# A diffusion-block kernel's head: x on the weights' queue, silu(c) and the norm factor in PSUM, fewer modulation tiles ahead of the first normed tile

## The chip, the cores and the metric

One core of one Trainium2 chip (trn2) runs the program. The metric is device microseconds of one execution, the median of several. Engines are called by their names or by the profile's short ones: TensorE (PE), VectorE (DVE), ScalarE (ACT), GpSimd (POOL), SyncE (SP, here only a DMA queue).

## What is computed

Two transformer blocks, one behind the other, on 512 tokens of width 1024, with a context of 256 tokens in the second. The head of the first block is what matters here:

```python
c_act = jax.nn.silu(c)
mod = c_act @ w_ada[l] + b_ada[l]
sh1, sc1, gt1, sh2, sc2, gt2 = [m[:, None, :] for m in jnp.split(mod, 6, axis=-1)]
h = rms_norm(x, g_norm1[l]) * (1.0 + sc1) + sh1
proj = h @ w_in[l]
qa, ka, va, qb, kb, vb, gates = jnp.split(proj, split_at, axis=-1)
```

`rms_norm` divides by the root of the mean square over the 1024 channels. Behind it come two attentions, gates, an output projection and a feed-forward part, then two further layers with their own modulation (`layer` 1 and 2 of the code).

## The kernel before

`build_program` writes a list of steps, `plan`, in one order. Each engine walks the whole list and issues its own part of each step, so an engine's order is the plan's order; waits on semaphores are placed from tokens that each step carries. x lies transposed in SBUF, channels on partitions: `XL` is 8 tiles of 128 channels x 512 tokens.

Products are made in three terms. Each weight unit of 128x1024 fp32 is loaded into one of three `RAW` buffers, ScalarE writes its rounded high part `SHI` (L2072), POOL the low part `SLO` (L2242), and TensorE issues high x high, high x low, low x high (L2505 to L2507). `with_splits` puts a unit's split into the plan: for the first three units at the places `first_splits`, which the head notes behind squares 1, 3 and 5, for later units where the buffer's former unit is released. `load_order` sorts what SyncE's queue issues: modulation tiles and weight units by a number `at`, plan positions for other transfers of that queue. At the start x, c and CONST (which holds the matrix of ones) go over ScalarE's queue, and tiles and units over SyncE's.

A **modulation tile** is 128 of the 6144 outputs of `c_act @ w_ada`. Its 128x1024 weights are loaded into `ADA` or `early` buffers, and one VectorE operation (L2321) multiplies them by the broadcast silu(c) and sums along the row, with a small read of the accumulator behind it. A pair of tiles, shift k and scale k, is wanted for channel tile k.

The head runs as follows. ScalarE makes silu(c) (L2067), then squares the eight x tiles (L2076), with the first three unit splits between them. TensorE sums all squares with a matrix of ones (L2497). ScalarE makes the factor r in two steps (L2080, L2082). `started` issues modulation pairs and then, for each k: `Coef` (L2326), `f = x * coef * r` (L2306, VectorE), `HLh` (L2086, ScalarE), and one step later `HLl` (L2311, VectorE). Then `v_tiles` multiplies: for each k, 4 token blocks x 3 terms, 96 instructions in all, two k to a weight unit. Its four banks are copied into `vb` (`VCopy`), two by ScalarE (L2091) and two by VectorE (L2332), and the query and key projections follow.

Pairs 0 to 4 are issued ahead of k = 0, and pair k + 5 ahead of `Coef` k for k = 0, 1, 2. Two pools of PSUM banks exist: 4 to 7 are handed out by `take`, 0 to 3 belong to the attention scores and are unused in the head.

## Time and profile before

| | us |
|---|---|
| median of 3 runs | 2798.8 (2796.88 to 2801.44) |
| profiled execution, its own time | 2794.1 |
| profiled execution, span | 2791.8 |
| TensorE busy | 2618.6 |
| VectorE, ScalarE, GpSimd busy | 1558.8, 1102.8, 983.8 |
| first instruction of the value projection | 39.75 |
| last instruction of it, start | 62.80 |

The profiled execution's own time contains 2.3 us outside its span. All times of day below are microseconds from the span's start. Busy time of a waiting engine's neighbours tells little: an engine's idle time matters only if TensorE, which is busy most of the span, waits for it.

### The profile page before, as it was taken

Reading aid. Unit: us, or ns where it says so; the run is one execution under the profiler, and the core shown is the slowest. Engines: PE = TensorE matmul, PEld = TensorE weight load, DVE = VectorE, ACT = ScalarE, POOL = GpSimd, SP = SyncE. Lnnn points to the kernel's source line nnn. Section 1 sums busy time; section 2 is a strip of 40 time slices with the busy share of each in tenths; the row PEclk is TensorE's granted clock in tenths of the full one; section 3 lists DMA queues with packets and bytes.
Section 4 is the critical chain, followed back from the end, with each engine's and each line's share of the span. In section 5 each row is a group of like instructions: output and inputs, shape, how many; then the busy total and the mean of one; then the engine's idle time right before and its main releaser. Section 6 shows DMA issues by size and latency. Waiting matters only on the chain. (4 is left out here: it accounts for less than half of the span.)

```text
span 2791.8 us, 39434 instructions
## 1 busy us (share of the span) xinstructions
PE 2618.6 (94%) x15254; PEld 2191.6 (78%) x15254; DVE 1558.8 (56%) x2430; ACT 1102.8 (40%) x2033; POOL 983.8 (35%) x564
## 2 busy tenths in 40 slices
PE   5997989999999989998899999999899997899998
PEld 3765678888888867776888888888788886788887
DVE  5445246654555355657766556556768677732224
ACT  3453342332322455555412112125656556522222
POOL 2245534444544411222332333332222122344444
PEclk9999999999999999999999999999999999999999
DMA  6644224443344100001234333321111111122222
GB/s 250 222 157 142 72 73 147 140 143 128 129 136 132 46 15 21 28 27 59 69 128 144 114 112 131 114 91 49 51 46 54 54 55 38 57 96 97 98 98 76
DMA packets 81608, 267.83 MB, mean 96 GB/s; under 512 B 8720, under 2 KB 16528, under 8 KB 81424
## 3 DMA queue, kind: packets, MB, share of 16 engines
q1 hardware_dynamic: 78000, 257.59, 27.6%
q10 hardware_dynamic: 3136, 6.42, 0.7%
q8 instruction: 122, 2.00, 0.3%
q0 software_dynamic: 288, 1.31, 0.1%
q14 instruction: 62, 0.51, 0.1%
HBM read 260.57 MB, written 4.72 MB: 95 GB/s over the span
## 5 line engine op out<-in xcount | busy, mean ns | idle before, releaser
L2242 POOL TENSOR_TENSOR SLO<-RAW,SHI 128x1024 fp32r<-128x1024 f32 (+1 forms) x291 | 708.4, 2437 | 1126.8 <-ACT SHI L2072 1121.4
L2072 ACT ACTIVATE SHI<-RAW 128x1024 fp32r<-128x1024 f32 (+1 forms) x335 | 345.5, 1035 | 1037.5 <-PE PS L2507 1030.1
L2505 PE MATMUL PS<-HLh,SHI 128*128 128x512 f32 (+1 forms) x1800 | 704.5, 391 | 13.3 <-POOL SLO L2242 5.6
L2507 PE MATMUL PS<-HLh,SLO 128*128 128x512 f32 (+1 forms) x1800 | 680.0, 378 | 0.0
L2506 PE MATMUL PS<-HLl,SHI 128*128 128x512 f32 (+1 forms) x1800 | 679.9, 378 | 0.0
L2505 PEld LDWEIGHTS PS<-HLh,SHI 128*128 128x128 f32 x1800 | 342.0, 190 | 84.6 <-issue 18.1
L2507 PEld LDWEIGHTS PS<-HLh,SLO 128*128 128x128 f32 x1800 | 341.4, 190 | 63.9
L2506 PEld LDWEIGHTS PS<-HLl,SHI 128*128 128x128 f32 x1800 | 342.4, 190 | 60.9 <-issue 6.1
L2505 PE MATMUL PS<-hh,SHI 128*128 128x512 f32 (+1 forms) x1016 | 366.5, 361 | 11.0 <-POOL SLO L2242 3.9
L2507 PE MATMUL PS<-hh,SLO 128*128 128x512 f32 (+1 forms) x1016 | 356.6, 351 | 0.0
L2506 PE MATMUL PS<-hl,SHI 128*128 128x512 f32 (+1 forms) x1016 | 355.0, 349 | 0.0
L2383 DVE SCALAR_TENSOR_TENSOR XL<-PS,MOD,XL 128x512 f32<-128x512 f32 (+1 forms) x328 | 215.0, 668 | 194.0 <-PE PS L2507 193.1
L2390 DVE TENSOR_TENSOR hl<-f,hh 128x512 fp32r<-128x512 f32 x88 | 165.0, 1875 | 122.6 <-ACT hh L2141 122.6
L2505 PEld LDWEIGHTS PS<-hh,SHI 128*128 128x128 f32 x1016 | 192.2, 189 | 47.8 <-issue 12.8
L2388 DVE TENSOR_TENSOR f<-f,PS 128x512 f32<-128x512 f32 x88 | 54.2, 616 | 301.1 <-PE PS L2507 281.8
L2506 PEld LDWEIGHTS PS<-hl,SHI 128*128 128x128 f32 x1016 | 192.3, 189 | 27.7 <-issue 1.2
L2507 PEld LDWEIGHTS PS<-hh,SLO 128*128 128x128 f32 x1016 | 192.3, 189 | 27.1
L2321 DVE CUSTOM_DVE_ANT_0 ADA<-ADA,cb,COL 128x1024 f32<-128x1024 f32 x96 | 181.4, 1889 | 0.0
L2505 PE MATMUL PS<-HCh,SHI 128*128 128x256 f32 x560 | 165.0, 295 | 13.6 <-DVE HCl L2311 7.5
L2506 PE MATMUL PS<-HCl,SHI 128*128 128x256 f32 x560 | 160.0, 286 | 0.0
L2507 PE MATMUL PS<-HCh,SLO 128*128 128x256 f32 x560 | 159.9, 286 | 0.0
L2321 DVE CUSTOM_DVE_ANT_0 cdump<-ADA,cb,COL 128x1024 f32<-128x1024 f32 x96 | 135.8, 1414 | 13.3 <-DMA ADA<-in_k_w 13.3
(257 smaller groups left out, 3929.3 us busy)
## 6 DMA issues: line engine op xcount, KB each, us to landing
RAW<-in_k_w SPq DMA_DIRECT2D x317, 512.0 KB, 3.5
ADA<-in_k_w SPq DMA_DIRECT2D x132, 512.0 KB, 4.3
early<-in_k_w SPq DMA_DIRECT2D x12, 512.0 KB, 18.7
RAW<-in_k_w SPq DMA_DIRECT2D x18, 256.0 KB, 2.6
XL<-in_xT ACTq DMA_DIRECT2D x4, 512.0 KB, 14.0
bi<-in_k_bias SPq DMA_DIRECT2D x16, 128.0 KB, 3.7
out<-XL SPq DMA_DIRECT2D x16, 128.0 KB, 1.8
bi<-in_k_bias SPq DMA_DIRECT2D x8, 192.0 KB, 4.0
```

Of the source, the lines that this page charges most:

```text
L2072: eng.activation(u.hi, u.w, ACT.Copy).then_inc(S["a_hi"], 1)
L2242: eng.tensor_tensor(u.lo, u.w, u.hi.bitcast(F32), ALU.subtract).then_inc(S["g_lo"], 1)
L2321: eng.tensor_tensor_reduce(w if j == n - 1 else st.dump, w, c, 1.0, st.bias, ALU.mult, ALU.add, st.mod[:, j:j + 1]).then_inc(S["v_ada"], 1)
L2383: eng.scalar_tensor_tensor(out=st.x, in0=st.src, scalar=st.gate, in1=st.x, op0=ALU.mult, op1=ALU.add).then_inc(S["v_res"], 1)
L2388: eng.tensor_tensor(st.f, st.f, st.src, ALU.mult).then_inc(S["v_up"], 1)
L2390: eng.tensor_tensor(st.lo, st.f, st.hi.bitcast(F32), ALU.subtract).then_inc(S["v_ulo"], 1)
L2505: eng.matmul(st.out, lh, rh, start=st.first and j == 0, stop=False)
L2506: eng.matmul(st.out, lh, rl, start=False, stop=False)
L2507: i = eng.matmul(st.out, ll, rh, start=False, stop=st.last and j == n - 1)
```

## The change

x goes over SyncE's queue: its first two transfers right behind COL, then the first two modulation tiles (`ADA`), then its other two, then early tiles and units mixed. The three first weight units move back in that queue. CONST comes second on ScalarE's queue, which has only c ahead of it. silu(c) is written to PSUM banks 0 and 1 instead of back into `c1`, and the modulation tiles of the head read it there, as first operand. The first norm's sums and its factor lie in bank 2. Only pairs 0 and 1 stand ahead of the loop, and pair k + 2 goes ahead of `Coef` k for k = 0 to 5. Behind the head, ScalarE copies silu(c) from PSUM back to `c1` for the remaining tiles of the layer. The operands of all modulation tiles change places.

```diff
--- before.py
+++ after.py
@@ -173,7 +173,7 @@
 Split = namedtuple("Split", "unit t_free")
 SplitLow = namedtuple("SplitLow", "unit")
 Setup = namedtuple("Setup", "t_col")
-Silu = namedtuple("Silu", "x t_in t_done")
+Silu = namedtuple("Silu", "x out t_in t_done")
 Square = namedtuple("Square", "x out acc n t_x t_free t_acc first on t_add")
 Rstd = namedtuple("Rstd", "acc sums bank t_bank t_mm t_ln t_rs")
 NormA = namedtuple("NormA", "x coef r out n t_in t_free t_done hi bias t_bias t_hfree t_hi")
@@ -393,7 +393,7 @@
 
         for u in units:
             before = units[u.k - NRAW] if u.k >= NRAW else None
-            u.at, u.t_free = (before.split_at, before.tok) if before else ((0.015, 0.035, 0.055)[u.k], None)
+            u.at, u.t_free = (before.split_at, before.tok) if before else ((6.535, 6.565, 6.595)[u.k], None)
         own = [(i, st) for i, st in enumerate(plan) if type(st) is Dma and st.queue == "sp"]
         return sorted([(u.at, u) for u in adas + units] + own[1:], key=lambda p: p[0])
 
@@ -540,7 +540,7 @@
         for row, c in zip(rows, cells):
             d = dma("act", c, t_in["k_crow"][row, :].partition_broadcast(128), wait)
             t = tick("a_cs")
-            put(Silu(c, d, t))
+            put(Silu(c, c, d, t))
             toks.append(t)
         return toks
 
@@ -999,11 +999,12 @@
     cdump = Cell(place("cdump", [128, USZ], F32, c_at + 8 * USZ)[:, :])
     c1 = place("c1", [128, USZ], F32, XC_at)[:, :]
     d_c1 = dma("act", c1, t_in["k_crow"][0, :].partition_broadcast(128))
-    d_xl = [dma("act", XL[:, 2 * NT * a:2 * NT * (a + 1)].rearrange("p (k n) -> p k n", k=2),
+    d_const = dma("act", CONST[:, :], t_in["k_const"])
+    d_xl = [dma("sp", XL[:, 2 * NT * a:2 * NT * (a + 1)].rearrange("p (k n) -> p k n", k=2),
                 t_in["xT"][256 * a:256 * a + 256, :].rearrange("(k p) n -> p k n", p=128)) for a in range(4)]
-    d_const = dma("act", CONST[:, :], t_in["k_const"])
-    cbc = {0: ([c1], [tick("a_cs")])}
-    put(Silu(c1, d_c1, cbc[0][1][0]))
+    cps = PS[:, 0:1024]
+    cbc = {0: ([cps], [tick("a_cs")])}
+    put(Silu(c1, cps, d_c1, cbc[0][1][0]))
     xl = [XL[:, NT * k:NT * k + NT] for k in range(8)]
     xc = [XC[:, NC * k:NC * k + NC] for k in range(8)]
     xl_rdy, xc_rdy = [[d_xl[k // 2]] for k in range(8)], [[] for _ in range(8)]
@@ -1037,10 +1038,11 @@
     stage = place("mstage", [128, 4224], F32, AR)
     first = [m for k in range(8) for m in (k, 8 + k)]
     early = slots([Cell(place(f"early{i}", [128, USZ], F32, AR + 4 * USZ * i)[:, :]) for i in range(12)])
-    for i, c in enumerate(early):
-        c.at = 0.01 * (i + 2)
+    for i, c in enumerate(ada_cells + early):
+        c.at = 4.5 if i < 2 else 6.5 + 0.01 * i
     loads = {m: ada_load(0, m, c) for m, c in zip(first, [None] * 2 + early)}
     st = Stats(NT, W)
+    st.bank = Cell(PS[:, 1024:1536])
     st.late, st.split = [*W["pt"].cells, *W["f"].cells], 1
     first_splits = []
     for k in range(8):
@@ -1076,12 +1078,12 @@
             for m in (k, 8 + k):
                 ada_tile(0, m, *(loads[m] if m in loads else ada_load(0, m)))
 
-        for k in range(5):
+        for k in range(2):
             pair(k)
         for k in range(9):
             if k < 8:
-                if k < 3:
-                    pair(k + 5)
+                if k < 6:
+                    pair(k + 2)
                 t_cf = tick("v_coef")
                 put(Coef(o[:, k:k + 1], MOD1[:, 8 + k:9 + k], col("g1", k), [mod_tok[(0, 8 + k)]]))
                 now = norm_tile(k, xl, xl_rdy, st.T, rs1, o[:, k:k + 1], t_cf, MOD1[:, k:k + 1], mod_tok[(0, k)], W, hl, [])
@@ -1095,6 +1097,10 @@
     coef_n[0] = 1
     toks = started()
     t_first = mod_tok[(0, 15)]
+    t_c1 = tick("a_vcopy")
+    put(VCopy("a", c1, cps, cbc[0][1], [], t_c1))
+    cbc[0] = ([c1], [t_c1])
+    scores.cells[0].free, scores.cells[1].free = [t_first, t_c1], st.bank.free
     for c in (W["va"].cells + W["qa"].cells + W["vb"].cells + W["qb"].cells + W["e"].cells):
         c.free = [t_first]
     MK = W["mk"].cells[0].ap.bitcast(BF16)
@@ -2064,7 +2070,7 @@
 
             def silu_c(st):
                 a.wait_ge(st.t_in)
-                eng.activation(st.x, st.x, ACT.Silu).then_inc(S["a_cs"], 1)
+                eng.activation(st.out, st.x, ACT.Silu).then_inc(S["a_cs"], 1)
 
             def split(st):
                 u = st.unit
@@ -2318,7 +2324,7 @@
                 for j, c in enumerate(st.cs):
                     if j < n - 1:
                         v.wait_ge(st.t_dfree)
-                    eng.tensor_tensor_reduce(w if j == n - 1 else st.dump, w, c, 1.0, st.bias, ALU.mult, ALU.add,
+                    eng.tensor_tensor_reduce(w if j == n - 1 else st.dump, c, w, 1.0, st.bias, ALU.mult, ALU.add,
                                              st.mod[:, j:j + 1]).then_inc(S["v_ada"], 1)
 
             def coef_(st):
```

On SyncE's queue the start read, ahead of the first load that waits (`XL` is x, `RAW` a weight unit, `early` and `ADA` modulation tiles):

```order
L2041 DMA COL<-in_k_cols 128x246
L2049 DMA ADA_55<-in_k_w 128x1024
L2049 DMA ADA_56<-in_k_w 128x1024
L2049 DMA RAW_57<-in_k_w 128x1024
L2049 DMA early_135<-in_k_w 128x1024
L2049 DMA early_136<-in_k_w 128x1024
L2049 DMA RAW_58<-in_k_w 128x1024
L2049 DMA early_137<-in_k_w 128x1024
L2049 DMA early_138<-in_k_w 128x1024
L2049 DMA RAW_59<-in_k_w 128x1024
L2049 DMA early_139<-in_k_w 128x1024
```

and now reads

```order
L2047 DMA COL<-in_k_cols 128x246
L2051 DMA XL<-in_xT 128x2x512 x2
L2055 DMA ADA_55<-in_k_w 128x1024
L2055 DMA ADA_56<-in_k_w 128x1024
L2051 DMA XL<-in_xT 128x2x512 x2
L2055 DMA early_135<-in_k_w 128x1024
L2055 DMA early_136<-in_k_w 128x1024
L2055 DMA RAW_57<-in_k_w 128x1024
L2055 DMA early_137<-in_k_w 128x1024
L2055 DMA early_138<-in_k_w 128x1024
L2055 DMA early_139<-in_k_w 128x1024
L2055 DMA RAW_58<-in_k_w 128x1024
```

The three units had 2, 4 and 6 modulation tiles ahead of them on this queue; they have 4, 7 and 10, and all of x. The third unit's row (`RAW_59`) stands behind `early_140` to `early_142`, past the last row shown.

On ScalarE the rows from the first square to the last now read (`r`, `f`, `pt` hold squares, `SHI` a unit's high part):

```order
L2082 ACTIVATE r_108<-XL 128x512 [waits s_d3]
L2082 ACTIVATE f_104<-XL 128x512
L2078 ACTIVATE SHI_60<-RAW_57 128x1024 [waits s_d_raw0]
L2082 ACTIVATE f_103<-XL 128x512 [waits s_d4]
L2082 ACTIVATE f_102<-XL 128x512
L2078 ACTIVATE SHI_61<-RAW_58 128x1024 [waits s_d_raw1]
L2082 ACTIVATE f_101<-XL 128x512 [waits s_d5]
L2082 ACTIVATE pt_107<-XL 128x512
L2078 ACTIVATE SHI_62<-RAW_59 128x1024 [waits s_d_raw2]
L2082 ACTIVATE pt_106<-XL 128x512 [waits s_d6]
L2082 ACTIVATE pt_105<-XL 128x512
```

Their order is that of before, and only the semaphores of x differ. Behind the projection ScalarE now has

```order
L2078 ACTIVATE SHI_60<-RAW_57 128x1024 [waits s_p_mm,s_d_raw0]
L2097 ACTIVATE c_78<-PS 128x1024 [waits s_a_cs]
L2097 ACTIVATE vb_84<-PS 128x512 [waits s_v_ada]
L2097 ACTIVATE vb_84<-PS 128x512
```

where the second row is new.

On VectorE the first normed tiles read before, from the twelfth modulation tile on (each `MOD_68 128x1` row is the read of the accumulator behind a tile):

```order
L2321 ISA early_144,MOD_68<-early_144,c_78,COL 128x1024 [waits s_d_ada54]
L2321 ISA MOD_68 128x1
L2326 SCALAR_TENSOR_TENSOR COEF<-MOD_68,COL 128x1 [waits s_v_ada]
L2306 SCALAR_TENSOR_TENSOR f_101<-XL,COEF,r_108 128x512 [waits s_d2,s_p_stat,s_v_coef,s_a_rs]
L2321 ISA early_145,MOD_68<-early_145,c_78,COL 128x1024 [waits s_d_ada55]
L2321 ISA MOD_68 128x1
L2321 ISA early_146,MOD_68<-early_146,c_78,COL 128x1024 [waits s_d_ada56]
L2321 ISA MOD_68 128x1
L2326 SCALAR_TENSOR_TENSOR COEF<-MOD_68,COL 128x1 [waits s_v_ada]
L2306 SCALAR_TENSOR_TENSOR f_102<-XL,COEF,r_108 128x512 [waits s_v_coef]
L2311 SCALAR_TENSOR_TENSOR HLl<-f_101,MOD_68,HLh 128x512 [waits s_v_nf,s_a_nhi]
```

and now, from the sixth tile on:

```order
L2327 ISA early_138,MOD_68<-PS,early_138,COL 128x1024 [waits s_d_ada48]
L2327 ISA MOD_68 128x1
L2332 SCALAR_TENSOR_TENSOR COEF<-MOD_68,COL 128x1 [waits s_v_ada]
L2312 SCALAR_TENSOR_TENSOR f_101<-XL,COEF,PS 128x512 [waits s_d3,s_p_stat,s_v_coef,s_a_rs]
L2327 ISA early_139,MOD_68<-PS,early_139,COL 128x1024 [waits s_d_ada49]
L2327 ISA MOD_68 128x1
L2327 ISA early_140,MOD_68<-PS,early_140,COL 128x1024 [waits s_d_ada50]
L2327 ISA MOD_68 128x1
L2332 SCALAR_TENSOR_TENSOR COEF<-MOD_68,COL 128x1 [waits s_v_ada]
L2312 SCALAR_TENSOR_TENSOR f_102<-XL,COEF,PS 128x512 [waits s_v_coef]
L2317 SCALAR_TENSOR_TENSOR HLl<-f_101,MOD_68,HLh 128x512 [waits s_v_nf,s_a_nhi]
```

Six tiles stand ahead of the first `f` instead of twelve, and the other ten behind it.

## Rows read from the trace of the kernel before

**Rows 1.** Part 1 of the page, busy time, share and instructions.

```profile
PE 2618.6 (94%) x15254; PEld 2191.6 (78%) x15254; DVE 1558.8 (56%) x2430; ACT 1102.8 (40%) x2033; POOL 983.8 (35%) x564
```

**Rows 2.** Waits of TensorE, 0 to 300 us: total, times, longest.

```profile
PE PS L2497 <- DMA CONST<-in_k_const: 23.7, 1, 23.7
PE PS L2513 <- ACT f L2095: 11.8, 7, 1.7
...
PE PS L2505 <- ACT vb L2091: 1.8, 1, 1.8
```

**Rows 3.** DMA view, 0 to 80 us: GB/s in 40 slices of 2 us.

```profile
GB/s 22 215 329 411 421 408 399 406 397 403 401 412 408 412 408 412 408 412 406 219 16 289 217 6 0 0 0 35 231 254 12 246 16 0 143 379 393 314 360 326
```

**Rows 4.** DMA issues, 0 to 40 us: count, size of each, median us to landing.

```profile
early<-in_k_w SPq DMA_DIRECT2D x12, 512.0 KB, 18.7
...
XL<-in_xT ACTq DMA_DIRECT2D x4, 512.0 KB, 14.0
...
c<-in_k_crow ACTq DMA_DIRECT2D x1, 512.0 KB, 5.2
CONST<-in_k_const ACTq DMA_DIRECT2D x1, 320.0 KB, 20.0
COL<-in_k_cols SPq DMA_DIRECT2D x1, 123.0 KB, 4.6
```

**Rows 5.** Timeline, 23 to 35 us: start, us, engine, line, [idle before].

```profile
23.87 1.06 ACT L2072 ACTIVATE SHI<-RAW 128x1024 fp32r<-128x1024 f32 x1 [3.80 <-DMA RAW<-in_k_w]
...
24.83 1.13 ACT L2076 ACTIVATE pt<-XL 128x512 f32<-128x512 f32 x2
...
25.13 3.30 DVE L2321 CUSTOM_DVE_ANT_0 early<-early,c,COL 128x1024 f32<-128x1024 f32 x1 [1.39 <-DMA early<-in_k_w]
...
27.29 0.34 PEld L2497 LDWEIGHTS PS<-f,CONST 128*128 128x128 f32 x1 [0.52 <-issue]
...
28.14 0.34 PEld L2497 LDWEIGHTS PS<-f,CONST 128*128 128x128 f32 x1 [0.52 <-issue]
```

**Rows 6.** Timeline, 23 to 35 us: the last sums and the norm factor.

```profile
30.76 2.74 PE L2497 MATMUL PS<-pt,CONST 128*128 128x512 f32 x6
...
33.54 0.69 ACT L2080 ACTIVATE r<-PS,SMALL 128x512 f32<-128x512 f32 x1 [7.58 <-PE PS L2497]
...
34.92 0.75 DVE L2306 SCALAR_TENSOR_TENSOR f<-XL,COEF,r 128x512 f32<-128x512 f32 x1 [0.38 <-ACT r L2082]
```

**Rows 7.** Timeline, 30 to 80 us: one step of VectorE after the first `f`.

```profile
35.59 1.28 DVE L2321 CUSTOM_DVE_ANT_0 early<-early,c,COL 128x1024 f32<-128x1024 f32 x1
...
38.19 0.75 DVE L2306 SCALAR_TENSOR_TENSOR f<-XL,COEF,r 128x512 f32<-128x512 f32 x1
...
39.52 1.28 DVE L2321 CUSTOM_DVE_ANT_0 ADA<-ADA,c,COL 128x1024 f32<-128x1024 f32 x1
```

**Rows 8.** Timeline, 30 to 80 us: the projection, and the fourth unit's split.

```profile
39.75 0.76 PE L2505 MATMUL PS<-SHI,HLh 128*128 128x512 f32 x1 [6.25 <-ACT HLh L2086]
...
42.82 0.39 PE L2506 MATMUL PS<-SLO,HLh 128*128 128x512 f32 x1
...
49.72 0.75 DVE L2306 SCALAR_TENSOR_TENSOR f<-XL,COEF,r 128x512 f32<-128x512 f32 x1
...
52.26 4.75 POOL L2242 TENSOR_TENSOR SLO<-RAW,SHI 128x1024 fp32r<-128x1024 f32 x2 [24.91 <-ACT SHI L2072]
...
62.80 0.39 PE L2507 MATMUL PS<-SHI,HLl 128*128 128x512 f32 x1
```

**Rows 9.** Stretches of 5 us: busy (instructions) by engine, granted clock, DMA, GB/s.

```profile
35.00:40.00 5.00, 0.25 (x1) 0.28 (x2) 4.96 (x9) 1.44 (x2) 0.00 (x0) 0.59 0.83 332
```

**Rows 10.** Timeline, 58 to 75 us: ScalarE behind the projection.

```profile
63.29 1.06 ACT L2072 ACTIVATE SHI<-RAW 128x1024 fp32r<-128x1024 f32 x1 [4.38 <-PE PS L2507]
```

**Rows 11.** Groups by form, VectorE, then ScalarE, whole span: busy, mean ns.

```profile
L2353 DVE CUSTOM_DVE_ANT_0 e<-PS,mk 128x768 f32<-128x768 f32 x16 | 14.7, 955 | 18.9 <-PE PS L2525 18.9
...
L2095 ACT ACTIVATE f<-PS 128x512 f32<-128x512 f32 x30 | 17.5, 584 | 12.0 <-PE PS L2507 12.0
```

## The prediction

> **What bounds the kernel now.** I read the page's part 1 first: TensorE is busy for 94% of the span [rows 1], so a microsecond counts only where it moves TensorE's work. The change touches the head alone, so I next read what TensorE waited for there. After CONST it waited 6.25 us for the first `HLh` tile [rows 8], and 1.8 us for a `vb` copy after the value projection [rows 2]. The reader is to see that everything before 39.7 us is latency, that the projection then runs without a gap, and that its end is followed by one ScalarE wait.
>
> What sets the first normed tile? The transfers run at 400 to 420 GB/s from about 6 to 38 us, so the head is a queue of bytes [rows 3, 4]. CONST, last on ScalarE's queue, lets the sums of squares start only at 23.7 [rows 2]; ScalarE meanwhile waits for the third weight unit at 23.87 and squares the last two x tiles behind it, until 25.96. TensorE's sums end at about 33.5 [rows 5, 6]. The norm factor follows, and VectorE starts the first `f` (I call this moment N) at 34.92. Twelve modulation tiles were done by then; VectorE was idle for only 0.38 us before it [rows 6], so sums and modulation tiles are nearly balanced.
>
> **Part 1, the transfers and N.** x lands early and CONST no longer holds the sums. But the three weight splits still stand between the squares on ScalarE, which works in order, and the change puts the third unit behind eight early tiles instead of four. Ahead of its landing now lie COL (123 KB), x (4x512), c (512), CONST (320), two ADA, eight early and three RAW tiles (13x512): 9659 KB, 9.89 MB [rows 4]. Before, the same count up to that unit gave 7.79 MB (nine tiles on SP, COL, and all of ScalarE's queue), and it landed at 23.87, when the slices of rows 3 add to 8.4 MB: a landing trails the bytes by 0.6 MB. So it now lands when they add to 10.5 MB: 10.09 MB at 28 us, and 0.4 MB more at 408 GB/s, is 29.0 us. The split takes 0.96 from start to start and the two squares 1.13 [rows 5]: the last square ends at 31.1.
>
> Each of the eight sums is two TensorE instructions. Early in the stage they follow each other at 28.14 - 27.29 = 0.85 us, at its end six take 2.74, 0.43 apart [rows 5, 6]: the chip's two levels, 1.2 and 2.4 GHz, one after the other in unbroken work. At full clock only the last sum is left behind the last square (the one before runs 30.55 to 31.4), and it ends at 32.3. From the last sum to N takes 34.92 - 33.54 = 1.4 [rows 6]: N = 33.7, **1.2 us earlier**. Bounds: with no lag of the landing, 1.5 us earlier still; with twice the lag 1.5 later; at half clock the last two sums end at 33.95 and N is 35.35 (a rival, below). By then VectorE has long done its six tiles: the sixth lands when 6587 KB and the lag, 7.35 MB, are through, at 21.3, and ends at 22.6. VectorE then idles for 11 us, and ten tiles are left for after N, where before there were four.
>
> **Part 2, the pace after N.** In the row before, a step with a pair takes 39.52 - 35.59 = 3.93 us (two tiles, coefficient, `f`, `HLl`) [rows 7]; a step without, 1.5 (3.93 less two tiles at 1.21, which with the 0.19 of the coefficient make 38.19 - 35.59). Five steps after the first tile now carry a pair, where two did. The first `HLl` comes as before at N + 4.7, and TensorE starts then. Its clock is low at that moment: 0.59 on average from 35 to 40 [rows 9], and the first seven instructions take from 39.75 to 42.82; from there 88 steps of 0.227 lead to the last one at 62.80 [rows 8]. Twelve instructions make a tile, so 2.7 us per tile against VectorE's 3.93: TensorE now waits 1.1 to 1.2 us for each of the tiles 2 to 4. Before, it never waited.
> The end is set by the last unit. The eighth `f` starts at N + 3.27 (34.92 to 38.19 before, which is 0.67 + two tiles + 0.19) + 4x3.93 + 2x1.52 = N + 22.0. From that `f` to POOL's low part of the fourth unit takes 52.26 - 49.72 = 2.5 (its `HLh`, the unit's split), and the low part 2.4 (two in 4.75) [rows 8]: N + 27.0. TensorE's last 24 instructions need it, 5.6 us with the drain: the projection ends at N + 32.6. Before: 62.80 + 0.39 = 63.2, N + 28.3. **4.3 us later.**
> A tile whose c lies in PSUM isn't in the trace. The nearest row with the same operation and one PSUM input is 955 ns for 768 columns, against 1.28 us for 1024 from SBUF [rows 7, 11]. 955 x 1024/768 is 1273, and if part of the 955 is a fixed cost it is less: with 0.15 fixed, 1223. So 0 to 0.05 less. Ten tiles: 0.5 us less, or nothing. I take nothing and keep 0.5 for the range. `f` reads its factor from PSUM at about the same price; also nothing.
> The Trainium skill ("VectorE: DVE Perf Modes", the section on the TRN2 errata) speaks against the change here: a PSUM source has 62 cycles more of fixed cost than an SBUF source. By it ten tiles would cost about 0.65 us more, an estimate from that page, and the sum would be 4.8. The row of this case contradicts it.
> The modulation tiles that ran beside POOL took up to 3.30 us [rows 5]; without the second SBUF input that should fall to 1.28. I cost it at nothing: all of these now stand in VectorE's new idle time. The Trainium skill ("SBUF — State Buffer", "SBUF: two separate sides") states the same lock between GpSimd and a VectorE operation with two SBUF inputs; by it the gain would be about 2 us per tile beside POOL, an estimate whose place is off the path.
>
> **Part 3, the copy of c.** ScalarE gets one more instruction, PSUM to SBUF, 1024 columns, between the split of the next unit, which starts at the projection's end at 63.29, and the `vb` copy for which TensorE waits [rows 2, 10]. A copy of 512 columns from PSUM takes 0.58 [rows 11], the split of 1024 takes 1.06 [rows 10]; I take **1.0**, bounds 0.9 and 1.1. It can't run ahead, since the split before it waits for the projection's end. The operand swap in the other modulation tiles and the changed bank numbers cost nothing: same shapes, same engines. Everything behind hangs on tokens of this stage, so the shift runs through to the end.
>
> **Sum:** -1.2 + 4.3 + 1.0 = **+4.1 us**. The profiled execution took 2794.1 (span 2791.8), so it would be 2798.2; the median of the runs shown is 2798.8, 0.17% above the profiled one, so I forecast **2802.9 us**, 0.15% slower. Below 0.2% (5.6 us) a measurement of this kernel can hardly tell it from no change.
>
> **Rivals.**
> *Half clock through the last sums, slower.* The sums now come in pairs with ScalarE's waits between, so TensorE may still be at 1.2 GHz when the last two start. For: before, the sums that began at 23.7 were still at the slow spacing after 28 us, with no wait between [rows 5]. Against: the waits are only some 1.7 us, behind pairs that take 3.4. It decides if both last sums run at 0.85 per instruction: N at 35.35, +1.65, in all +5.8: 2804.6, just slower. Chance 0.27. If the clock also fell in the 1.2 us gaps of the projection, each tile would cost 5.1 us, some 13 in all (2812). The low level of rows 9 came where TensorE had been idle since 33.5, five times as long as such a gap. Chance 0.04.
> *The squares are not held, faster.* If ScalarE had the units in time, the last x would land at 4.72 MB, 14.7 us, the sums run out at about 23 and N comes at 24.4: -10.5 + 4.3 + 1.0 = -5.2, and with the 0.5 of the PSUM tiles -5.7: 2793.1. It needs the third unit before 18 us, which the bytes forbid; the squares would have to be ahead of the splits. With everything that I don't see, 0.10.
> *The change is hidden.* If TensorE had other waits behind the head that absorb the delay, the result is within 1 us. But its waits for `f` (11.8 us in the first 300) [rows 2] are for copies of its own results, so 0.07.
> The forecast's own case has the rest, 0.52.
>
> **Numbers.** Faster 0.10. Same: the forecast's case less a sixth that its bounds put above 5.6, the hidden one, half of the half-clock case: 0.60. Slower 0.30. The range reaches from 2798.5 (hidden, or N 1.5 earlier with the cheaper tiles and a fast median) to 2808 (half clock, late landing, slow median).
>
> **What would show it.** Third split starting at 29.0; TensorE's sums in pairs with gaps; N at 33.7 (35.35 with slow sums); steps of 3.9 us on VectorE after N, and waits of TensorE for `HLl` or `HLh` of about 1.2; the projection's end at 66.3; tiles of 1.22 to 1.28 with no slow ones beside POOL; a wait of 2.8 instead of 1.8 behind the projection. N before 30, or a projection without gaps, would make me wrong.

## The result, and the profile after

| | before | after |
|---|---|---|
| median of 20 runs, us | 2798.36 (2794.16 to 2801.44) | 2803.43 (2797.91 to 2809.3) |
| ratio | | 1.0018 [1.0012, 1.0024] |
| profiled execution (span), us | 2794.1 (2791.8) | 2802.42 (2800.4) |

The change costs 5.07 us; 2802.9 was forecast. The interval of the ratio lies wholly above 1, so the loss is shown, and on both sides of the 0.2% that the prediction took for its bound. The line numbers of the program have moved by 6: `f` is L2312, `HLh` L2092, `HLl` L2317, the high parts L2078, the low parts L2248, the sums L2503, the tiles L2327.

Part 1 of the page, the answer to [rows 1]:

```profile
PE 2627.5 (94%) x15254; PEld 2195.9 (78%) x15254; DVE 1550.1 (55%) x2430; ACT 1103.0 (39%) x2034; POOL 985.7 (35%) x564
```

ScalarE has one instruction more, the copy of c. VectorE is 8.7 us less busy, and the program is slower all the same: its busy time was not what counted.

TensorE's waits in the first 300 us (total, times, longest), the answer to [rows 2]:

```profile
PE PS L2503 <- ACT f L2082: 8.9, 2, 7.6
PE PS L2503 <- ACT r L2082: 8.7, 1, 8.7
PE PS L2511 <- ACT HLh L2092: 8.0, 3, 6.2
...
PE PS L2503 <- ACT pt L2082: 3.1, 1, 3.1
...
PE PS L2511 <- ACT vb L2097: 2.7, 1, 2.7
...
PE PS L2511 <- POOL SLO L2248: 0.7, 1, 0.7
```

The 23.7 us for CONST are gone, and in their place stand four waits for squares, 20.7 us in all: TensorE takes a pair of sums and waits for the next. New as well are two waits for `HLh` within the projection (8.0 less the first one of 6.2) and one for the fourth unit's low part. The wait for `vb` has grown by 0.9.

From the view of transfers, 0 to 40 us, the answer to [rows 4]:

```profile
XL<-in_xT SPq DMA_DIRECT2D x4, 512.0 KB, 8.6
...
CONST<-in_k_const ACTq DMA_DIRECT2D x1, 320.0 KB, 6.4
```

x lands 8.6 us after its issue instead of 14.0, CONST 6.4 instead of 20.0: the first part of the change does what it says.

The timeline from 18 to 35 us (start, us, engine, line, [idle before]), ScalarE, TensorE and VectorE up to the first `f`, the answer to [rows 5, 6]:

```profile
18.39 1.06 ACT L2078 ACTIVATE SHI<-RAW 128x1024 fp32r<-128x1024 f32 x1 [9.31 <-DMA RAW<-in_k_w]
...
23.51 1.06 ACT L2078 ACTIVATE SHI<-RAW 128x1024 fp32r<-128x1024 f32 x1 [3.02 <-DMA RAW<-in_k_w]
...
25.14 1.12 PE L2503 MATMUL PS<-f,CONST 128*128 128x512 f32 x2 [1.34 <-ACT f L2082]
...
28.63 1.06 ACT L2078 ACTIVATE SHI<-RAW 128x1024 fp32r<-128x1024 f32 x1 [3.02 <-DMA RAW<-in_k_w]
29.59 1.13 ACT L2082 ACTIVATE pt<-XL 128x512 f32<-128x512 f32 x2
...
30.26 3.18 PE L2503 MATMUL PS<-pt,CONST 128*128 128x512 f32 x4 [3.14 <-ACT pt L2082]
...
33.48 0.66 ACT L2086 ACTIVATE PS<-PS,SMALL 128x512 f32<-128x512 f32 x1 [2.75 <-PE PS L2503]
...
34.79 0.75 DVE L2312 SCALAR_TENSOR_TENSOR f<-XL,COEF,PS 128x512 f32<-128x512 f32 x1 [12.48 <-ACT PS L2088]
```

x is in SBUF early, yet two squares still stand behind each split, and each split behind its unit's landing: 9.31, 3.02 and 3.02 us of waiting. The last four sum instructions take 3.18 us, 0.8 each, where the pair at 25.14 took 1.12. VectorE stands idle for 12.48 us ahead of `f`, where it was 0.38 [rows 6].

The timeline from 36 to 71 us, VectorE's steps, TensorE's waits and ScalarE's copy, the answer to [rows 7, 8, 10]:

```profile
38.05 0.75 DVE L2312 SCALAR_TENSOR_TENSOR f<-XL,COEF,PS 128x512 f32<-128x512 f32 x1
...
41.98 0.75 DVE L2312 SCALAR_TENSOR_TENSOR f<-XL,COEF,PS 128x512 f32<-128x512 f32 x1
...
51.38 0.47 PE L2511 MATMUL PS<-SHI,HLh 128*128 128x512 f32 x1 [0.94 <-ACT HLh L2092]
...
56.78 0.75 DVE L2312 SCALAR_TENSOR_TENSOR f<-XL,COEF,PS 128x512 f32<-128x512 f32 x1
...
59.31 7.09 POOL L2248 TENSOR_TENSOR SLO<-RAW,SHI 128x1024 fp32r<-128x1024 f32 x3 [27.20 <-ACT SHI L2078]
...
61.75 0.50 PE L2511 MATMUL PS<-SHI,HLh 128*128 128x512 f32 x1 [0.72 <-POOL SLO L2248]
...
67.09 0.39 PE L2513 MATMUL PS<-SHI,HLl 128*128 128x512 f32 x1
...
68.54 1.01 ACT L2097 ACTIVATE c<-PS 128x1024 f32<-128x1024 f32 x1
...
70.18 0.47 PE L2511 MATMUL PS<-HLh,SHI 128*128 128x512 f32 x1 [2.70 <-ACT vb L2097]
```

A step of VectorE is 41.98 - 38.05 = 3.93 us, and TensorE now waits for it (0.94 at 51.38, as much once more at 55.31). The eighth `f` comes at 56.78 instead of 49.72, the fourth low part at 59.31 instead of 52.26, and the query projection starts at 70.18. In the trace of before it started at 64.97, so the head costs **5.21 us** in these two traces.

TensorE's granted clock (its low level is 0.50, 1.2 GHz; its full level 1.00, 2.4 GHz), from the view of stretches of 5 us (busy and instructions of PE, PEld, DVE, ACT, POOL, then the clock, DMA share, GB/s):

```profile
25.00:30.00 5.00, 1.98 (x4) 0.68 (x4) 0.00 (x0) 1.98 (x4) 2.23 (x2) 1.00 1.04 413
30.00:35.00 5.00, 3.18 (x4) 0.86 (x4) 0.21 (x1) 1.97 (x4) 2.12 (x1) 0.59 1.03 410
35.00:40.00 5.00, 0.39 (x1) 0.42 (x2) 4.96 (x9) 1.44 (x2) 0.00 (x0) 0.50 0.82 327
40.00:45.00 5.00, 5.00 (x14) 3.85 (x14) 4.96 (x10) 0.72 (x1) 0.00 (x0) 0.54 0.00 0
```

Ahead of the last four sum instructions TensorE was idle for 3.14 us, and most of their time was at the low level: the granted clock is 0.95 from 30 to 31 us and 0.50 from 31 to 32. The four at 25.14 to 27.1, ahead of that wait, ran at the full level.

**Behind the head.** Subtracting the start of each matrix instruction from that of the same number in the other trace, the shift is 5.21 at 65 us, stays between 5.04 and 5.22 until 1300 us, and then grows by 1.4 us near 1343 us and by some 1.0 twice, near 1903 and near 2000 us; it is 8.55 at the end. All three jumps lie where the clock is low in one trace and not in the other. The first of them, a landmark that both traces have and then the stretch behind it, first of before and then of after (TensorE's busy time and instructions, the clock, DMA share, GB/s):

```profile
1337.17 0.55 PE L2505 MATMUL PS<-HCh,SHI 128*128 128x256 f32 x1 [6.38 <-DVE HCl L2311]
...
1343.00:1348.00 5.00, 4.29 (x34) 0.98 0.32 108
```

```profile
1342.23 0.55 PE L2511 MATMUL PS<-HCh,SHI 128*128 128x256 f32 x1 [6.37 <-DVE HCl L2317]
...
1348.00:1353.00 5.00, 4.23 (x22) 0.66 0.33 105
```

The landmark itself is 5.06 us later. In the stretch behind it, shifted by 5 us as the work is, before has a clock of 0.98 and 34 instructions, after 0.66 and 22. It is the same at the other two: 1.00 from 1903 to 1906 us in before, 0.50 from 1908.2 to 1911.2 in after; 1.00 from 2005.5 to 2009, 0.50 from 2010.5 to 2014. The profiled execution of before (2794.1) lies at the low end of its runs, and 3.3 of the 8.6 us by which the spans differ are these jumps. The medians differ by 5.07.

### The profile page after: what moved, and what is told of

Its sections match the earlier page's. It is cut to its first block and busy times, and to the rows that moved or that the text cites. A ratio compares the mean times of both kernels' runs of the same rounds, so it can differ in the third digit from the quotient of the medians.

```text
span 2800.4 us, 39437 instructions
## 1 busy us (share of the span) xinstructions
PE 2627.5 (94%) x15254; PEld 2195.9 (78%) x15254; DVE 1550.1 (55%) x2430; ACT 1103.0 (39%) x2034; POOL 985.7 (35%) x564
## 5 line engine op out<-in xcount | busy, mean ns | idle before, releaser
L2248 POOL TENSOR_TENSOR SLO<-RAW,SHI 128x1024 fp32r<-128x1024 f32 (+1 forms) x291 | 709.7, 2442 | 1132.0 <-ACT SHI L2078 1126.6
L2078 ACT ACTIVATE SHI<-RAW 128x1024 fp32r<-128x1024 f32 (+1 forms) x335 | 345.3, 1035 | 1043.8 <-PE PS L2513 1028.3
L2513 PEld LDWEIGHTS PS<-hh,SLO 128*128 128x128 f32 x1016 | 192.2, 189 | 27.1
L2327 DVE CUSTOM_DVE_ANT_0 ADA<-cb,ADA,COL 128x1024 f32<-128x1024 f32 x96 | 177.2, 1846 | 0.0
L2327 DVE CUSTOM_DVE_ANT_0 cdump<-cb,ADA,COL 128x1024 f32<-128x1024 f32 x96 | 135.6, 1413 | 14.5 <-DMA ADA<-in_k_w 14.5
```

What stands on the lines that cost most here:

```text
L2078: eng.activation(u.hi, u.w, ACT.Copy).then_inc(S["a_hi"], 1)
L2248: eng.tensor_tensor(u.lo, u.w, u.hi.bitcast(F32), ALU.subtract).then_inc(S["g_lo"], 1)
L2327: eng.tensor_tensor_reduce(w if j == n - 1 else st.dump, c, w, 1.0, st.bias, ALU.mult, ALU.add, st.mod[:, j:j + 1]).then_inc(S["v_ada"], 1)
L2513: i = eng.matmul(st.out, ll, rh, start=False, stop=st.last and j == n - 1)
```

## The experiments

**Terms of a ledger.** In each trace N is the start of the first `f`, and Q that of the query projection. The experiments were made to take one term away at a time; "held" is explained with the fourth of them. Medians are of 11 runs for each kernel of an experiment, and of 33 or 21 runs of the kernel before on the same chip; those of after and of its before are of 20. N and Q come from one profiled execution of each kernel.

| kernel | N | Q | Q - N | median minus before's, us | ratio |
|---|---|---|---|---|---|
| before | 34.92 | 64.97 | 30.05 | | |
| after | 34.79 | 70.18 | 35.39 | +5.1 | 1.0018 [1.0012, 1.0024] |
| five pairs ahead | 35.27 | 66.81 | 31.54 | +2.8 | 1.0009 [1.0, 1.0017] |
| c in SBUF | 33.67 | 68.18 | 34.51 | +4.5 | 1.0017 [1.0009, 1.0026] |
| copy early | 33.84 | 68.32 | 34.48 | +3.1 | 1.0012 [1.0003, 1.0021] |
| squares first | 22.48 | 60.50 | 38.02 | -3.2 | 0.9984 [0.9975, 0.9993] |
| before, two pairs | 34.16 | 68.71 | 34.55 | +2.7 | 1.0007 [0.9999, 1.0016] |
| sums filled up | 34.88 | 70.28 | 35.40 | +4.5 | 1.0016 [1.0006, 1.0025] |
| squares first, copy early | 22.73 | 59.82 | 37.09 | -6.1 | 0.9978 [0.9969, 0.9987] |
| projection woven in | 22.57 | 61.85 | 39.28 | -3.3 | 0.9986 [0.9977, 0.9995] |
| units behind x | 26.75 | 62.14 | 35.39 | -1.2 | 0.9994 [0.9985, 1.0003] |
| all three | 25.19 | 61.37 | 36.18 | -3.5 | 0.9989 [0.998, 0.9998] |

**1. Five pairs ahead again.** Only the pace goes back to that of before.

```diff
-        for k in range(2):
+        for k in range(5):
             pair(k)
...
-                if k < 6:
-                    pair(k + 2)
+                if k < 3:
+                    pair(k + 5)
```

> The changed kernel with five pairs of modulation tiles ahead of the first normed tile, as before, instead of two; all else of the change stays. My theory (VectorE's pace behind the first f costs 4.4 us): the first f (N) stays at 34.8, since the twelfth tile lands near 31.1 and is done by 32.4; the projection again runs without waits except for the start, ends at N + 28.3 = 63.1, and the query projection begins 2.7 later at 65.8, 4.4 earlier than in the changed kernel and 0.8 later than before. Time: 0.8 us above before (0 to 1.5). If the cost of the change is not this pace but the clock or the later stages, the time stays 4 to 6 us above before while the head's rows move.

It took 2799.93 (before: 2797.12). The projection ran without a wait again, from 40.08 to a last instruction at 63.73, N + 28.5, where after has N + 32.3. Q - N fell by 3.85. The time was missed by 2 us (0.8 above before was expected), and Q by 1.0. N was 0.47 late. The projection, without a wait in both, took 0.6 longer than in before, since the clock rose later: it was 0.56 on average from 40 to 45 us, and 0.73 in before. A low stretch of the clock that before doesn't have followed at 69 us; whether it accounts for the rest isn't shown. Timeline, the last sums and the norm factor:

```profile
30.43 3.49 PE L2503 MATMUL PS<-pt,CONST 128*128 128x512 f32 x4 [3.14 <-ACT pt L2082]
...
33.96 0.66 ACT L2086 ACTIVATE PS<-PS,SMALL 128x512 f32<-128x512 f32 x1 [3.06 <-PE PS L2503]
```

The last four sum instructions took 3.49, 0.87 each: the low level but for the start of the first (0.88 from 30 to 31 us, 0.50 from 31 to 34). This is the rival of the half clock, with N at 35.27 (35.35 was its price).

**2. The pace alone, on the kernel before.**

```diff
-        for k in range(5):
+        for k in range(2):
             pair(k)
...
-                if k < 3:
-                    pair(k + 5)
+                if k < 6:
+                    pair(k + 2)
```

> The kernel before with one part of the change alone: two pairs of modulation tiles ahead of the first normed tile. Theory: the sums end at 33.5 whatever VectorE does, so N stays at 34.9; VectorE idles before it and its steps of 3.93 set the pace, the projection ends at N + 32.6 = 67.5 and the query projection begins at 69.3, 4.3 later than before. Time: 4.3 us above before, all that the change costs except the copy. Rival (the cost comes from the new transfer order or from PSUM): within 1 us of before.

2800.88 (before: 2798.15). Q - N is 34.55, **4.5** more than in the kernel before with no other edit; with run 1 the pace is worth 3.85 to 4.5 us (4.3 in the prediction), and the 0.6 between the two is run 1's later rise of the clock. The wait for `HLh` came three times and the one for the fourth low part once, 0.7, as in after. N came 0.76 earlier than in the profile of before: CONST landed at 23.2 instead of 23.7, and the sums reached the full level one instruction sooner. VectorE was idle for 10.71 us ahead of the first `f`. The median rose by 2.7 where 4.3 was expected, and its interval includes no change: that the pace costs something is read from the traces, not from the times.

**3. c in SBUF; the copy early.** Silu in place and no copy at all:

```diff
-    cps = PS[:, 0:1024]
-    cbc = {0: ([cps], [tick("a_cs")])}
-    put(Silu(c1, cps, d_c1, cbc[0][1][0]))
+    cbc = {0: ([c1], [tick("a_cs")])}
+    put(Silu(c1, c1, d_c1, cbc[0][1][0]))
...
-    t_c1 = tick("a_vcopy")
-    put(VCopy("a", c1, cps, cbc[0][1], [], t_c1))
-    cbc[0] = ([c1], [t_c1])
-    scores.cells[0].free, scores.cells[1].free = [t_first, t_c1], st.bank.free
+    scores.cells[1].free = st.bank.free
```

> The changed kernel with silu(c) left in SBUF and no copy of it behind the head. Theory: tiles beside POOL take 2.5 to 3.3 us again, but in VectorE's idle time, so N stays at 34.8 and the projection's end at 67.5; TensorE waits 1.8 instead of 2.7 behind it, and the time falls by 0.9 us, to 4.2 above before. Rival (PSUM is needed for the tiles): the six tiles end later than 34 us, or the steps of 3.93 us grow, and the time does not fall or rises.

And the tiles from PSUM as in after, with the copy right behind the silu:

```diff
-    cbc = {0: ([cps], [tick("a_cs")])}
-    put(Silu(c1, cps, d_c1, cbc[0][1][0]))
+    t_cs, t_c1 = tick("a_cs"), tick("a_vcopy")
+    cbc = {0: ([cps], [t_c1])}
+    put(Silu(c1, cps, d_c1, t_cs))
+    put(VCopy("a", c1, cps, [t_cs], [], t_c1))
...
-    t_c1 = tick("a_vcopy")
-    put(VCopy("a", c1, cps, cbc[0][1], [], t_c1))
```

> The changed kernel with ScalarE's copy of silu(c) from PSUM to SBUF moved right behind silu, and the first tile waiting for the copy. Theory: it lies in ScalarE's idle time of 9 us and costs nothing there; N stays at 34.8, the wait behind the projection is 1.8 instead of 2.7 us, the time falls by 0.9, as in the run with c in SBUF, to 4.2 above before. If the copy of 1.0 us is not on the path, nothing changes.

2801.57 and 2800.2 (before: 2797.12). Q - N is 34.51 and 34.48: **0.9** less than in after both times, and TensorE's wait for `vb` is 1.8 again. So the copy costs 0.9 at its place and nothing when early, and the tiles' reading from PSUM costs nothing by itself. The medians (+4.5 and +3.1, with +5.1 for after) have intervals too wide to show 0.9; this too is read from the traces. The kernel with c in SBUF, timeline:

```profile
19.61 2.35 POOL L2244 TENSOR_TENSOR SLO<-RAW,SHI 128x1024 fp32r<-128x1024 f32 x1 [19.16 <-ACT SHI L2074]
19.77 3.27 DVE L2323 CUSTOM_DVE_ANT_0 early<-c,early,COL 128x1024 f32<-128x1024 f32 x1 [1.27 <-DMA early<-in_k_w]
...
25.23 2.07 PE L2499 MATMUL PS<-f,CONST 128*128 128x512 f32 x2 [1.34 <-ACT f L2078]
27.09 1.92 PE L2499 MATMUL PS<-pt,CONST 128*128 128x512 f32 x2
...
30.34 1.98 PE L2499 MATMUL PS<-pt,CONST 128*128 128x512 f32 x4 [1.34 <-ACT pt L2078]
```

The tile beside POOL takes 3.27 us, not 1.28, and VectorE's idle time swallows it. In this execution the last four sums ran at full level (1.98 for four), so that N came at 33.67, the forecast's 33.7; with the copy early it was the same (1.98) and N was 33.84. The level at the pairs before was the low one (2.07 and 1.92), and in after it was the other way round.

**4. Squares first.** The splits of the first three units go behind all squares, behind the norm factor and behind the first `HLh`: the prediction's rival "the squares are not held".

```diff
-        if k in (1, 3, 5):
-            first_splits.append(len(plan))
+    first_splits.append(len(plan))
     rs1 = rstd(st)
+    first_splits.append(len(plan))
...
+                if k == 0:
+                    first_splits.append(len(plan))
```

> The changed kernel with all eight squares ahead of the three weight splits on ScalarE (the second split behind the norm factor, the third behind the first HLh). Theory (the third unit's landing at 28.6 holds N): the last square ends near 16, the sums near 20.5 to 23, N is 22.4 to 24.5; then VectorE's steps follow the landings of the tiles, pair 7 lands near 40, the eighth f starts near 44.5, the projection ends near 55 and the query projection begins near 57.7: 7 us under before and 12 under the changed kernel, 2791 us. Rival (the sums or the DMA order hold N anyway, or the later stages take the gain back): N above 30, or a time within 2 us of before.

2793.88 (before: 2797.12), faster, by 3.2, where 7 was expected. N came at 22.48, 12.3 us earlier than in after. But Q came only 9.7 earlier. Timeline:

```profile
24.70 2.35 POOL L2250 TENSOR_TENSOR SLO<-RAW,SHI 128x1024 fp32r<-128x1024 f32 x1 [2.77 <-ACT SHI L2080]
24.86 1.28 DVE L2329 CUSTOM_DVE_ANT_0 early<-PS,early,COL 128x1024 f32<-128x1024 f32 x1 [0.43 <-DMA early<-in_k_w]
26.07 1.00 DVE L2334 SCALAR_TENSOR_TENSOR COEF<-MOD,COL 128x1 f32<-128x1 f32 x1
...
29.82 2.38 POOL L2250 TENSOR_TENSOR SLO<-RAW,SHI 128x1024 fp32r<-128x1024 f32 x1 [2.77 <-ACT SHI L2080]
30.84 1.38 DVE L2334 SCALAR_TENSOR_TENSOR COEF<-MOD,COL 128x1 f32<-128x1 f32 x1
```

A coefficient, one element per partition, took 1.00 and 1.38 us instead of 0.15. Each ended 0.02 us behind POOL's low part (27.07 against 27.05, 32.22 against 32.20). It reads two operands from SBUF, the tile beside it reads c from PSUM and took 1.28 as ever. So VectorE lost 0.43 to a landing and 0.85 + 1.23 to these two, 2.51 in all: this is "held". 38.02 less 2.51 is 35.5, after's own 35.39. The expectation's Q of 57.7 left this out.

**5. Sums filled up.** Three more products of the sixth square go between the sums, into an unused bank, so that TensorE has more to do. They change no output.

```diff
+                    if j == 5 and st is head_sum:
+                        for _ in range(3):
+                            eng.matmul(PS[:, 1536:2048], ones, x, start=True, stop=True)
```

> The changed kernel with three more products of the ones matrix with the sixth square, into an unused bank, behind the sixth sum on TensorE; they do no work for the result. They fill the wait of 3.1 us before the last two sums. Theory (in the changed kernel's profile the last two sums ran at the low level, 0.8 us per instruction, because TensorE had waited): the last two run at 0.43, the norm factor starts near 32.4 instead of 33.5 and N is 33.7, the query projection begins near 69.1, and the time is 4.1 above before. If the level has nothing to do with the wait, the last sums take 3.2 us again and N stays at 34.8.

2802.63 (before: 2798.15), N at 34.88. Timeline:

```profile
28.83 2.98 PE L2508 MATMUL PS<-pt,CONST 128*128 128x512 f32 x6
...
31.65 1.88 PE L2505 MATMUL PS<-pt,CONST 128*128 128x512 f32 x4
```

**Inconclusive.** The pairs of sums ahead ran at the low level in this execution, and the clock rose at 29.3, during the first of the six added instructions (0.50 up to 29, 0.84 from 29 to 30, 1.00 behind). The last four sums ran at full level (1.88), but so they did in both runs of 3, which have no added products and whose clock was full again from 29 to 29.5 on. The added ones ended only at 31.8, behind the last square's 30.8, and so the last four, which started at 30.34 and 30.50 in the runs of 3, started at 31.65. What decides the level here wasn't found out.

**6. Squares first and copy early**, edits 3 (second) and 4 together.

> Squares ahead of the splits and the copy of c right behind silu, both together. The two costs lie at different places of the path, so they add: N at 22.5, the query projection begins at 59.6 (60.5 less 0.9), 5.4 earlier than before; time 0.9 under the run with the squares first, about 4.1 us under before. If they don't add, the time is that of the run with the squares first, 3.2 under before.

**2792.07** (before: 2798.15), the lowest ratio of all, though its interval overlaps those of runs 4, 7 and 9, and by the two ratios 0.4% (11 us) below after. The shift was 6.1, where 4.1 was expected. Q fell by 0.7 from run 4, N being 0.25 later. Q - N is 37.09; less the 2.5 that VectorE is held (coefficients of 1.00 and 1.39, a landing of 0.43) it is 34.6, as in both kernels of 3. The longer of the two, 31.09 to 32.48, ended with POOL's low part at 32.47.

**7. The projection woven in.** On top of 6, each channel tile's products stand right behind its `HLl`, so that the fourth and fifth units' splits come earlier in ScalarE's order.

```diff
                 norm_low(*late, W, hl, hl_rdy, [])
+                toks = v_tiles(late[0])
             late = now
-        for k in range(8):
-            toks = v_tiles(k)
```

> As the run before in this list, and the projection's steps stand in the plan right behind the HLl of their channel tile, so that the units four to six are split between the normed tiles and not behind the last. Theory: the wait of TensorE for POOL's low part of the fourth unit goes (the projection's end hung on the last f by 2.5 + 2.4 + 5.6 us); the last tile's HLl is at 48.4, the last 24 instructions start then or when TensorE is through with tile 5 near 50, the projection ends near 55.3 and the query projection begins near 57.2, 2.4 earlier than in the run before; time near 2790.5, 6.5 under before. Rival: POOL's low parts now lie beside VectorE's steps and hold its coefficients and HLl, up to 2.4 us each time, and the sixth unit's split holds the last HLh: the gain is under 1 us.

2794.87 (before: 2798.15): 2.8 us above kernel 6, though the two intervals overlap. Q is 2.0 later, where 2.4 earlier was expected; the mechanism is that of the expectation's rival, which had priced it at a gain under 1 us and not at a loss. Timeline:

```profile
46.65 2.41 POOL L2249 TENSOR_TENSOR SLO<-RAW,SHI 128x1024 fp32r<-128x1024 f32 x1 [5.84 <-ACT SHI L2079]
47.22 2.39 DVE L2318 SCALAR_TENSOR_TENSOR HLl<-f,MOD,HLh 128x512 fp32r<-128x512 f32 x1 [0.17 <-ACT HLh L2093]
...
52.86 1.06 ACT L2079 ACTIVATE SHI<-RAW 128x1024 fp32r<-128x1024 f32 x1 [5.04 <-PE PS L2514]
```

POOL's low parts now ran beside VectorE's `HLl`, which also reads two tensors from SBUF and took 2.39 instead of 0.75; and the last split waited 5.04 us for TensorE with the last `HLh` behind it on ScalarE. Work moved ahead in an in-order queue brought its own wait along.

**8. Units behind x.** Instead of moving the splits, the three units are loaded right behind x, and the plan stays that of after.

```diff
-            u.at, u.t_free = (before.split_at, before.tok) if before else ((6.535, 6.565, 6.595)[u.k], None)
+            u.at, u.t_free = (before.split_at, before.tok) if before else ((6.505, 6.508, 6.511)[u.k], None)
```

> The changed kernel with one thing moved: the three weight units are loaded directly behind x, ahead of the early tiles. The splits stay between the squares. Theory (only the landing of the third unit holds the squares): it lands near 18.6 instead of 28.6, the last square is done by 20.8 and the sums by about 23; now the sixth modulation tile, at 24 to 25, sets N at 25.2; steps of 3.93 then give the eighth f at 47.3, the projection's end at 57.9 and the query projection at 60.6, 4.4 earlier than before and 9.6 earlier than in the changed kernel. Time: 3 to 4 us under before. Rival (something else of the change holds N, such as PSUM or the sums' own length): N above 30.

2795.68 (before: 2796.88), where 3 to 4 us under before was expected; the interval includes no change. The traces say more. Timeline:

```profile
20.14 1.04 ACT L2078 ACTIVATE SHI<-RAW 128x1024 fp32r<-128x1024 f32 x1
...
22.67 2.74 PE L2503 MATMUL PS<-pt,CONST 128*128 128x512 f32 x6
...
26.75 0.75 DVE L2312 SCALAR_TENSOR_TENSOR f<-XL,COEF,PS 128x512 f32<-128x512 f32 x1 [1.55 <-ACT PS L2088]
```

The third split starts at 20.14 and no longer waits, and N falls from 34.79 to 26.75. **This is the proof of the prediction's first step:** every compute engine has after's order, only SyncE's loads differ, and with the units' landings out of the way the squares, the sums and N come 8 us earlier. The edit moves all three units, but in after the third split was the last to wait (28.63), ahead of the last two squares. N was 1.5 later than expected, and it was the sums again that set it, not the sixth tile, whose coefficient was done at 25.2: the last twelve sum instructions ran from 17.78 to 25.4 without a break, the first five at the low level, 0.85 apiece. Q - N is 35.39, after's to the hundredth, and here no coefficient meets POOL, whose three low parts end at 24.3.

**9. All three**, edits 3 (second), 4 and 8 together.

> Squares first, copy early and units behind x together. Theory: VectorE's own work (16 tiles at 1.2 us, eight steps at 1.5) is the bound once N lies near 25, whatever brings it there. N comes at 25.3, later than the 22.7 of the run with squares first and copy early, but no coefficient waits for POOL now; the eighth f is at 47.3 and the query projection begins at 59.7, as in that run (59.8). Time within 1 us of it, 6 us under before. If N itself were what counts, it would be 2.6 us slower.

2793.41 (before: 2796.88), Q at 61.37, 1.55 later than in kernel 6. N is 25.19, 2.46 later; VectorE is held by one coefficient instead of two. Timeline:

```profile
27.72 2.34 POOL L2250 TENSOR_TENSOR SLO<-RAW,SHI 128x1024 fp32r<-128x1024 f32 x1 [4.07 <-ACT SHI L2080]
...
28.27 1.81 DVE L2334 SCALAR_TENSOR_TENSOR COEF<-MOD,COL 128x1 f32<-128x1 f32 x1
```

28.27 + 1.81 = 30.08, again 0.02 behind POOL. 36.18 less the 1.66 that it lost is 34.52. The expectation had N right (25.3) and Q at 59.7, with no coefficient waiting for POOL; Q's miss of 1.67 is the one coefficient that did.

With these the ledger closes for all kernels but two: Q = N + 30.05 (head of before), + 4.4 for the pace, + 0.9 for the copy at its place, + what VectorE is held. Less the last of these, the four kernels of 3, 6 and 9, which have no copy there, give 34.5 to 34.6, and after, 4, 5 and 8, which have it, 35.4 to 35.5. Run 1 is 0.6 over its sum (the clock, above), and the woven plan of run 7 isn't one of these sums. The medians follow Q's shift within 1.7 us.

## Why the prediction was right

The forecast was 2802.9, the median 2803.43, the shift +4.1 against +5.07 (medians) and +5.21 (Q of the traces). So the shift was missed by 1.0; that the time was missed by only 0.5 is luck, since the median of before fell from 2798.8 to 2798.36 with more runs. Of the terms -1.2, +4.3 and +1.0 the last two came true, as +4.4 and +0.9, and the first came as -0.1.

**Part 1, N.** The order of events was right and so was its cause. The third split came at 28.63 (29.0), the last squares ended at 30.7 (31.1). The size failed: 1.2 us earlier was forecast, 0.13 was measured in after's profile. The term mis-sized is "at full clock only the last sum is left": the last two sums took 3.18 us, at mixed level. The argument against the half clock, waits of "only some 1.7 us, behind pairs that take 3.4", held the slow pairs for given; in after the pair took 1.98 at the full level, and the wait behind it was 3.14. The rival's N of 35.35 was seen in run 1 (35.27), the forecast's 33.7 in the runs of 3 (33.67, 33.84), and after's profile lies between. The prediction had the two as alternatives for the kernel, with 0.52 and 0.27. The four profiles, of kernels with the same TensorE work up to there, suggest rather that an execution may meet either, and that a median sees a mixture. That isn't shown: each is one execution of another kernel, and neither the change within one kernel nor the share of each was measured.

**Part 2, the pace.** Right: VectorE's steps of 3.93, the eighth `f` at N + 22.0 (56.78), the projection's end at N + 32.7 (67.09 + 0.39) where N + 32.6 was written, so +4.4 for +4.3. One detail was off: TensorE waited only twice for `HLh` and once for POOL, 2.6 us in all, and not for each of the tiles 2 to 4; its first twelve instructions, at the low level (seven before), filled the earlier gaps.

**Tiles from PSUM.** Cost nothing, as taken. All tiles of after with either source, from the view of the tiles' line (ns min/median/max):

```profile
L2327 DVE CUSTOM_DVE_ANT_0 ADA<-c,ADA,COL x32: 1266/1284/3414, 69.7 to 302.9; 128x1024 f32<-128x1024 f32 x32
L2327 DVE CUSTOM_DVE_ANT_0 early<-PS,early,COL x12: 1275/1280/1284, 15.8 to 48.4; 128x1024 f32<-128x1024 f32 x12
```

A tile from PSUM takes 1275 to 1284 ns and one from SBUF has a median of 1284. The 62 cycles that the Trainium skill ("VectorE: DVE Perf Modes", the section on the TRN2 errata) adds for a PSUM source are not seen. The maxima show the other side, 3414 ns with c in SBUF and never with c in PSUM; the Trainium skill's rule of the lock between GpSimd and a VectorE operation with two SBUF inputs ("SBUF — State Buffer", "SBUF: two separate sides") agrees, and the coefficients of runs 4, 6, 7 and 9 fit it as well.

**Part 3, the copy.** 1.0 was forecast, 1.01 is the instruction, and 0.9 is the price: `vb` starts 0.90 behind it, and taking it away gives 0.9 in two kernels.

**Rivals.** "Hidden" is out: the shift of 5.2 us is still there at 1300 us. "Not held", the rival on the other side, was the true mechanism of another kernel: it needs the splits or the units moved (runs 4 and 8), as the prediction said. It priced N at 24.4; 22.48 and 26.75 came. The whole was priced at -5.2 and came as -3.2 (run 4) and -1.2 (run 8, with an interval that includes no change). It had no term for VectorE being held by POOL once N comes that early.

**The bound of 0.2%.** The prediction held that below it a measurement can hardly tell a change from none. With 20 runs of each the interval of the ratio is 0.12% to 0.24% above 1: a loss of 0.18% was told from none.

## What to carry to other kernels

- An engine that works in order holds a chain by its other input. CONST and x came 14 and 5 us earlier here and N moved by 0.1, since a weight unit's landing stood between the squares; name the last-landing input of every instruction ahead of the one that you speed up.
- Work moved from ahead of a wait to behind it costs its full price if that engine sets the pace behind the wait. Six tiles fewer ahead of N bought 12 us of idle time on VectorE and cost 4.4 us.
- Put helper copies where their engine is idle: the same instruction cost 0.9 us between a split and a copy that TensorE waits for, and nothing 60 us earlier.

## What the runs showed that was not expected

- A VectorE instruction of 128x1 elements with two SBUF inputs, 0.15 us otherwise, took 0.84 to 1.81 us while POOL wrote a low part, and ended 0.01 to 0.02 us behind it in all eight cases in the heads of runs 4, 6, 7 and 9.
- The same last four sums took 1.98, 3.18 and 3.49 us in three kernels that do not differ up to there in what they issue on TensorE: what the granted level does to them differs between these three executions by 1.5 us, more than the forecast's first term.
- Low stretches of the clock far behind the head differ between executions of nearly the same program, and each moves the end by 1 to 1.4 us. With head edits of 3 to 5 us, the shift at Q is free of them, though it still holds the luck of the clock within the head (1.5 us in N, 0.6 in the projection); the median of many runs averages over both.
